# Memory attention in a two-layer decoder step: score halves in two PSUM banks, one score slot, and the sample items' value product turned round

## The reference

```python
def memory_attention(q, mk, mv):
    s = jnp.einsum('bqhd,bmhd->bhqm', q, mk, preferred_element_type=jnp.float32) * (MEM_HEAD_DIM ** -0.5)
    p = jax.nn.softmax(s, axis=-1)
    return jnp.einsum('bhqm,bmhd->bqhd', p.astype(mv.dtype), mv)

# in every layer
z = rmsnorm(x) @ w_in[l]
z_mix, z_mem = z[..., :MIX_WIDTH], z[..., MIX_WIDTH:]
mix = pooling(z_mix) @ w_pool        # layer 0
mix = differential_attention(z_mix)  # layer 1
x = x + concat(mix, memory_attention(z_mem)) @ w_out[l]
x = x + relu(rmsnorm(x) @ w_mlp1[l])**2 @ w_mlp2[l]
```

## Time and profile before

| | |
|---|---|
| three runs, us | 1315.67, 1316.85, 1321.41 (median 1316.85) |
| profiled execution, us | 1317.09 |
| its span, us | 1315.2 |
| PE busy | 1245.6 us, 95% |
| PE weight loads busy | 1192.0 us, 91% |
| DVE busy | 588.8 us, 45% |
| ACT busy | 406.6 us, 31% |
| POOL busy | 355.8 us, 27% |

### The profile page before, as it was taken

How to read it: one execution, slowest core, us unless ns; L and a number is a source line. 1 busy time by engine, 2 the same in 40 slices (tenths; PEclk the granted TensorE clock), 3 DMA queues, 4 the chain that set the end, 5 groups by cost and what they waited for, 6 DMA issues and landing times.

```text
span 1315.2 us, 23409 instructions
## 1 busy us (share of the span) xinstructions
PE 1245.6 (95%) x9612; PEld 1192.0 (91%) x9612; DVE 588.8 (45%) x867; ACT 406.6 (31%) x750; POOL 355.8 (27%) x290
## 2 busy tenths in 40 slices
PE   6999899999999999999999988789999999999995
PEld 6888799999999999998889954589999999999994
DVE  7666554333333323356434787755332333333334
ACT  7433443212212212233322265633221212221221
POOL 4252023403404404421018010002511511511523
PEclk9988899999999999999889988889999999999997
DMA  7610522222222222222243266212222222222211
GB/s 273 235 52 20 178 90 81 86 91 81 97 81 91 84 96 80 80 97 80 81 132 106 66 239 206 100 48 82 97 81 83 94 91 86 80 96 80 95 48 68
DMA packets 37032, 132.57 MB, mean 101 GB/s; under 512 B 4226, under 2 KB 5122, under 8 KB 36322
## 3 DMA queue, kind: packets, MB, share of 16 engines
q1 hardware_dynamic: 35858, 123.42, 27.7%
q0 software_dynamic: 1104, 8.15, 2.1%
HBM read 121.18 MB, written 7.03 MB: 97 GB/s over the span
## 4 chain that ended last, share of the span: by engine, by line
PE 88%; DVE 7%; ACT 2%; issue 1%; DMA 0%; DVEq 0%; POOL 0%; SPq 0%; ACTq 0%
PE psum L425 79%; PE psum L560 2%; PE psum L474 1%; DVE inv_rms L1014 1%; DVE weights_split L995 1%; PE psum L565 1%; ACT weights_split L742 1%; DVE tiny L1102 1%; PE psum L490 1%; PE psum L527 1%; PE psum L501 1%; PE psum L547 1%; PE psum L505 0%; PE psum L521 0%; DVE probs_heads L1081 0%
## 5 line engine op out<-in xcount | busy, mean ns | idle before, releaser
L425 PE MATMUL psum<-operand_b,weights_split 128*128 128x272 f32 x4416 | 565.6, 290 | 4.0 <-DVE weights_split L995 3.8
L425 PEld LDWEIGHTS psum<-operand_b,weights_split 128*128 128x128 f32 x4416 | 560.4, 190 | 7.0 <-DVE weights_split L995 4.4
L425 PE MATMUL psum<-operand_a,weights_split 128*128 128x272 f32 (+1 forms) x4116 | 533.2, 292 | 24.2 <-DVE weights_split L995 18.3
L425 PEld LDWEIGHTS psum<-operand_a,weights_split 128*128 128x128 f32 x4116 | 527.5, 192 | 28.2 <-issue 20.9
L742 ACT ACTIVATE weights_split<-weights_raw 128x1024 fp32r<-128x1024 f32 (+1 forms) x186 | 192.6, 1036 | 430.6 <-PE psum L425 430.6
L995 DVE TENSOR_TENSOR weights_split<-weights_raw,weights_split 128x1024 fp32r<-128x1024 f32 (+1 forms) x186 | 239.1, 1285 | 136.1 <-ACT weights_split L742 136.1
L1380 POOL TENSOR_TENSOR squares<-staging 128x544 f32<-128x544 f32 x64 | 76.4, 1193 | 471.2 <-ACT operand_b L788 207.5
L1049 DVE TENSOR_TENSOR residual<-psum,residual 128x544 f32<-128x544 f32 x48 | 34.8, 725 | 175.8 <-PE psum L425 175.8
L1030 DVE SCALAR_TENSOR_TENSOR staging<-psum,inv_rms 128x544 f32<-128x544 f32 x56 | 40.6, 725 | 150.0 <-PE psum L425 150.0
L1373 POOL TENSOR_TENSOR squares_sum<-squares_sum,squares 128x544 f32<-128x544 f32 (+1 forms) x35 | 48.5, 1386 | 115.7 <-ACT squares L754 115.1
L1382 POOL TENSOR_TENSOR operand_a<-squares,operand_a 128x544 fp32r<-128x544 f32 x32 | 65.0, 2030 | 2.5
(11 more groups left out here) (198 smaller groups left out, 754.9 us busy)
## 6 DMA issues: line engine op xcount, KB each, us to landing
weights_raw<-in_weights SPq DMA_DIRECT2D x180, 512.0 KB, 3.6
cache_tiles<-in_page_k SPq DMA_DIRECT2D x16, 384.0 KB, 4.1
cache_tiles<-in_page_v SPq DMA_DIRECT2D x16, 384.0 KB, 3.7
cache_tiles<-in_mem_k SPq DMA_DIRECT2D x8, 512.0 KB, 4.6
cache_tiles<-in_mem_v SPq DMA_DIRECT2D x8, 512.0 KB, 5.5
residual<-in_x SPq DMA_DIRECT2D x1, 2176.0 KB, 11.6
out_y<-projected SPq DMA_DIRECT2D x8, 272.0 KB, 2.1
rotated<-projected POOLq DMA_DIRECT2D x4, 408.0 KB, 7.0
```

Of the source, the lines that this page charges most:

```text
L425: mm = pe.matmul(ps[:, 2 * (j % PS) + hf, 0:n], w(wr), act[:, ar, k, hf * n:(hf + 1) * n], start=(q == 0 and wr == 0 and ar == 0), stop=(q ...
```

## The change

- The two heads of a mem item are scored into bank 4 and bank 5, and `half_scored` is gone. Every item, memdec too, now has the one slot of both banks, so scores of item n wait for exp of item n-1.
- In a step PE mixes item `at`-1 before it scores item `at`+2; it scored first before. Scores of item 1 move from the middle of unit 2 to behind its end.
- `mix` of a mem item takes its four products in another order, so that neighbours write different halves of the partitions.
- `mix` of a memdec item has probabilities as weights (32 columns) and values as moving operand (256 columns): 8 matmuls instead of 16. The result stands the other way round, so ACT copies it (128x256) and PE turns it with two transposes at three quarters of the unit (`memdec_turn`); DVE drains it from there. Its `mixed` semaphore comes from these transposes.
- The second memdec item moves from place 6 to place 5.

```diff
-    items.insert(6, ("memdec", 1, 0))
+    items.insert(5, ("memdec", 1, 0))
...
             if n < FIRST_HEAD:
-                return ps[:, 4 + n % 2, :].rearrange("p (j k) -> p j k", j=2)
+                return ps[:, 4:6, :]
...
-                if n >= slots(n):
-                    pe.wait_ge(exped, n - slots(n) + 1)
+                if n >= FIRST_HEAD + SLOTS:
+                    pe.wait_ge(exped, n - SLOTS + 1)
+                elif n > FIRST_HEAD:
+                    pe.wait_ge(exped, FIRST_HEAD)
+                elif n:
+                    pe.wait_ge(exped, n)
                 if kind == "mem":
                     for hh in range(2):
                         lane = slice(64 * hh, 64 * hh + 64)
-                        if hh:
-                            pe.wait_ge(half_scored, QT * (MEM_PAIRS * l + a) + i + 1)
-                        mm = pe.matmul(sc[:, hh, 0:MEM], Z[lane, 6 + a, i * P:(i + 1) * P],
-                                       memKT[lane, l, a, :], start=True, stop=True)
-                        if hh == 0:
-                            mm.then_inc(half_scored, 1)
+                        mm = pe.matmul(sc[:, hh, 0:MEM], Z[lane, 6 + a, i * P:(i + 1) * P], memKT[lane, l, a, :],
+                                       start=True, stop=True)
...
-                    for hh in range(2):
-                        for kt in range(2):
+                    for kt in range(2):
+                        for hh in range(2):
...
-                    for b in range(4):
-                        c = chunk_of(n) + b // 2
-                        chunk_ready(pe, v_loaded, c)
-                        for pr in range(MEM_PAIRS):
-                            out = (pr * 4 + b) * 32
-                            for kt in range(2):
-                                at = (b % 2) * 512 + kt * MEM + pr * P
-                                mm = pe.matmul(ps[:, m0, out:out + 32], kv[:, c % 2, 1, at:at + P],
-                                               pt[:, kt * P + 32 * b:kt * P + 32 * b + 32],
-                                               start=(kt == 0), stop=(kt == 1))
+                    for o in range(2):
+                        chunk_ready(pe, v_loaded, chunk_of(n) + o)
+                    for kt in range(2):
+                        for b in range(4):
+                            at = (b % 2) * 512 + kt * MEM
+                            mm = pe.matmul(ps[32 * b:32 * b + 32, m0, 0:MEM], pt[:, kt * P + 32 * b:kt * P + 32 * b + 32],
+                                           kv[:, (chunk_of(n) + b // 2) % 2, 1, at:at + MEM],
+                                           start=(kt == 0), stop=(kt == 1))
+                    mm.then_inc(memdec_mixed, 1)
+                    return
...
+            def memdec_turn(n):
+
+                pe.wait_ge(memdec_copied, MEMDEC.index(n) + 1)
+                for pr in range(MEM_PAIRS):
+                    mm = pe.transpose(ps[:, 7, MEM + pr * P:MEM + (pr + 1) * P], memdec_rows(n)[:, pr * P:(pr + 1) * P],
+                                      ident)
+                mm.then_inc(mixed, 1)
...
                 turn(n0 + at)
+                if at:
+                    mix(n0 + at - 1)
                 if at + 2 < L0_ITEMS:
                     scores(n0 + at + 2)
-                if at:
-                    mix(n0 + at - 1)
...
+                if n0 + at - 1 in MEMDEC:
+                    n = n0 + at - 1
+                    act.wait_ge(memdec_mixed, MEMDEC.index(n) + 1)
+                    act.activation(memdec_rows(n), ps[:, 7, 0:MEM], ACT.Copy).then_inc(memdec_copied, 1)
```

More of the change, by code:

```diff
@@ L233, in build @@
         squared, clamped = sem("squared"), sem("clamped")
-        half_scored = sem("half_scored")
         new_mixed, new_added = sem("new_mixed"), sem("new_added")
         decode_mixed, decode_copied = sem("decode_mixed"), sem("decode_copied")
+        memdec_mixed, memdec_copied = sem("memdec_mixed"), sem("memdec_copied")
         sub_mean = sem("sub_mean")
@@ L310, in build, with memdec_rows @@
         DEC = [n for n, it in enumerate(ITEMS) if it[0] in ("memdec", "decode")]
+        MEMDEC = [n for n, it in enumerate(ITEMS) if it[0] == "memdec"]
+        def memdec_rows(n):
+            return T[:, n % 2, MEM:2 * MEM]
         DECODE = [n for n, it in enumerate(ITEMS) if it[0] == "decode"]
@@ L409, in _, with unit @@
         def _(pe):
-            def unit(u, j, act, kts=tuple(range(KT)), cols=TOK, ready=None, base_kt=0, first=False, mid=None):
+            def unit(u, j, act, kts=tuple(range(KT)), cols=TOK, ready=None, base_kt=0, first=False, mid=None, late=None):
                 pe.wait_ge(weight_lo, u + 1)
@@ L421, in unit @@
                         mid()
+                    if late and q == 3 * len(kts) // 4:
+                        late()
                     w = lambda r: split[:, j % HL, r, lo_of(k - base_kt)]
@@ L628, in memory_step, with after_memdec @@
             def memory_step(n0, at):
-                if at == "start":
-                    scores(n0)
-                    scores(n0 + 1)
-                    return
                 turn(n0 + at)
+                if at:
+                    mix(n0 + at - 1)
                 if at + 2 < L0_ITEMS:
                     scores(n0 + at + 2)
-                if at:
-                    mix(n0 + at - 1)
+            def after_memdec(n0, j):
+                n = n0 + 2 * (j - 3) - 1
+                return (lambda: memdec_turn(n)) if n in MEMDEC and j >= 4 else None
             for j in range(KT):
-                mid = (lambda: memory_step(0, "start" if j == 2 else 2 * (j - 3))) if j >= 2 else None
-                unit(U_IN0 + j, j, B, ready=normed(G_IN0) if j == 0 else None, mid=mid)
+                mid = (lambda: scores(0) if j == 2 else memory_step(0, 2 * (j - 3))) if j >= 2 else None
+                unit(U_IN0 + j, j, B, ready=normed(G_IN0) if j == 0 else None, mid=mid, late=after_memdec(0, j))
                 if j == 0:
@@ L654, in _ @@
                 if j == 2:
+                    scores(1)
                     pe.wait_ge(memv_ready, 2)
@@ L668, in _ @@
             for j in range(KT):
-                mid = (lambda: memory_step(L0_ITEMS, "start" if j == 2 else 2 * (j - 3))) if j >= 2 else None
-                unit(U_IN1 + j, j, A, ready=normed(G_IN1) if j == 0 else None, mid=mid)
+                mid = (lambda: scores(L0_ITEMS) if j == 2 else memory_step(L0_ITEMS, 2 * (j - 3))) if j >= 2 else None
+                unit(U_IN1 + j, j, A, ready=normed(G_IN1) if j == 0 else None, mid=mid, late=after_memdec(L0_ITEMS, j))
                 if j == 0:
@@ L673, in _ @@
                 if j == 2:
+                    scores(L0_ITEMS + 1)
                     pe.wait_ge(root_ready, R_IN1 + 1)
@@ L1121, in items_drain @@
                         for pr in range(MEM_PAIRS):
-                            grid = ps[lane, 7, P * pr:P * pr + P].rearrange("p (b c) -> p b c", b=4)
+                            grid = ps[lane, 7, MEM + P * pr:MEM + P * pr + P].rearrange("p (b c) -> p b c", b=4)
                             src = grid[:, :, 8 * pr + 4 * hh:8 * pr + 4 * hh + 4]
```

## The result

| | before | after |
|---|---|---|
| median of 19 runs each, us | 1320.75 (1314.12 to 1324.97) | 1309.26 (1306.15 to 1314.17) |
| ratio, 95% interval | | 0.9927 (0.9912 to 0.9942) |
| profiled execution and span, us | 1317.09, 1315.2 | 1310.02, 1308.2 |
| PE busy, us | 1245.6 | 1224.7 |
| mean granted clock of that execution | 0.969 | 0.971 |

The kernel became faster by 0.73%, some 9.6 us, where 16.3 were forecast (the two medians lie 11.5 us apart, the two profiled executions 7.1). In the profiled executions PE works 21 us less but the span is only 7.0 us shorter.

What follows compares the result with a forecast made beforehand. PE was taken to bound the kernel during the eight units of `w_in`. -21.5 - 12.0 + 14.2 + 3.0 = -16.3 us against the profiled 1317.1 gave 1300.8, range 1293 to 1310.

Steps and rivals of the forecast that it cites:

- What bounds it: During the eight units of `w_in` PE is the bound; its unit matmuls hold 79% of the span.
- Part 1: Memdec mix: 8 matmuls at 1.02 us and no clock drop save 5.38 us per item, 21.5 for four.
- Part 2: Mem item scores: halves overlap in two banks, saving 0.75 us for each of 16 items, 12.0 in all.
- Part 3: Waits of PE's scores for ACT's exp, added by the one slot, in both layers' items: 14.2 us together.
- step 2's mix: Layer 0, step 2: the mix, now first, waits 0.5 us for DVE's drain of item 0.
- the 0.8 of layer 0's step 0: Layer 0, step 0: PE waits 0.8 us for ACT's exp of item 1, behind DVE's work.
- The 0.2 us to spare in the middle steps: Layer 0's even steps: exp is ready only 0.2 us before PE arrives, so no wait.
- Part 4: Clock falls behind two of layer 1's four waits of about 2 us, 1.5 us each: 3.0 added.
- The mem mix at nothing: New order of the mem mix costed at nothing; it could give up to 5 us over 16 items.
- the rivals: No clock falls 0.20; falls behind most waits 0.10; halves don't overlap 0.06; middle steps wait 1 us 0.10, 2.8 us 0.04.
- the slow rival: Middle steps' scores wait 2.8 us or more each in both layers, making it slower by 0.5%, 1323.4 us; chance 0.04.
- the 2x of the page: Skill page's two-way row tiling speedup for mem scores: item from 1.38 to 0.69, 11.0 us in all, time 1301.9.

Runs made afterwards that it cites:

- The mix alone: Changed kernel with 15 small matmuls at PE's start and the old scoring (slots, half wait, order) restored, new memdec mix kept: 1296.08 us, ratio 0.9817.
- the score side alone: Kernel before with score halves in two banks, one slot, mix ahead of scores, item 1 scored behind unit 2; old memdec mix: 1310.24 us, ratio 0.991.

## Why the prediction was right in its parts and off in its sum

- **What bounds it.** Right: in the items' stretches what left PE's rows left the span.
- **Part 1, -21.5.** Right. The mix costs 1.00 us (1.02 forecast), no stretch at 1.2 GHz begins in it, and the half unit with the turn in it takes 3.33 (3.13 + 0.31 forecast). Mix and half unit came from 9.84 to 4.33, 5.5 per item. The mix alone measured -24 us in the runs, and in its item stretches -22.0.
- **Part 2, -12.0.** Right: 0.63 us per item for 0.64 forecast.
- **Part 3, +14.2.** Slightly high: the brackets are 4.3 in layer 0, 7.4 in layer 1 and 0.5 at step 2's mix, 12.1 together. A bracket begins at the modelled end of the row before, which lies 0.07 behind what that row costs, so the nine waits cost 12.8. Every odd step waits, and each bracket is 0.16 or 0.17 below its forecast. What did not come is the 0.8 of layer 0's step 0. The 0.2 us to spare in the middle steps was enough. With the old mix beside it the same part costs 9.5, so it holds only for the two sides together.
- **Part 4, +3.0.** Right in the profiled execution: two falls of 3.4 us in layer 1, 1.5 us each, at 608.4 and 645.9, behind one wait of 1.95 and one of 1.73; the other two of the same lengths brought none. It is not a constant: the same kernel run again had one such fall in layer 1, the one with 15 matmuls two, the one with the old mix order three.
- **The mem mix at nothing.** Right, by the run with the old order.
- **The sum.** This is the step that failed: "-21.5 - 12.0 + 14.2 + 3.0 = -16.3. Against the profiled execution, 1317.1" takes all that lies outside the items as unchanged, a term put at nothing without a reason. In the item stretches the profile shows -18.1, near what the parts as measured make (-22.0 - 12.0 + 12.8 + 3.0 = -18.2). Outside them the second MLP's loop gave back 7.0 us, and it had no term, no bound and no rival. With the loop at another place the same change measures a ratio of 0.9857, where 1300.8 of 1317.1 is 0.9876: 18.9 us less than its own before for 16.3 forecast. (That its 1301.15 us stand so near the 1300.8 is luck, since its before is 1318.5.) The traces of before could have warned: its instruction queue brought no packet in the second and third pass of either loop, and the change removes 108 instructions ahead of the second one.
- **The clock elsewhere.** The heads and the output took 5.6 us more in the profiled execution. This I cannot put down to the change: time at 1.2 GHz in that stretch was 41 us after and 27 before, but 44 in the kernel before with early exp and 17 to 48 in the others that carry the change (48 in the same changed kernel run again). In the runs as a whole the changed kernel spends less time at 1.2 GHz than before, not more.

None of the rivals happened. The range 1293 to 1310 held the median of 1309.26 only at its edge, by a cause that it did not contain, and that is luck. Two small slips of the working changed nothing: with the wake-up of 0.15 the slow rival needs ACT 4.7 us later and not 4.9, and the time by the 2x of the page is 1301.8 and not 1301.9. What stays open is what decides whether the clock falls behind a wait of 1.7 to 1.95 us, where the runs of the score side alone won more than their items show, and why the loop's bad range lies where it lies.

## What to carry to other kernels

A change that removes or adds instructions ahead of a hardware loop can move the loop's code to a place where, as here, each pass waits for instruction packets: compare the instruction queue's packets and the branches' times of both traces before any difference is put down to the edit, and pad PE's stream by a few matmuls to see. When two buffers are made into one, look at the reader's place in its engine's order: here the second slot had hidden that exp stood behind a weight rounding, and moving exp gave 14 us where the whole rest of the change gave 17. The two sides of this change weren't additive, since the old mix covered some of the score side's waits and both touched the clock, so each is to be measured beside the other, not only alone.

## What the runs showed of the hardware that was not expected

- A backward branch of PE over 1578 instructions costs 0.21 to 0.25 us or 3.7 to 4.8 us, by the loop's place. The slow form costs 7 us for two passes. Fifteen small matmuls more made the program 8 us faster.
- In the kernel before the clock fell to 1.2 GHz in each of the four mixes of 16 matmuls with 32 moving columns, 1.9 to 2.6 us after the mix began and for 6.8 us, although PE showed busy throughout; these mixes took 4.7 to 5.4 us. It is not fixed: with early exp on ACT and PE's order as before, one of the four took 3.78 us with 3.4 at 1.2 GHz behind it and another 5.93 with 10.2. With the score side alone changed all four took 3.7 to 3.9, and the stretches were 3.4, 6.8, 0 and 3.4 us. What makes the difference is open.
- The spread of one kernel's runs is mostly clock: over 17 runs of the kernel before, spans and mean clocks correlate at -0.97. The span grows by 0.32 us for each us at 1.2 GHz, and beside that line the spans spread by only 0.75 us (standard deviation; 3.2 without it).
